# Expert weights of a one-core encoder step: 16 KB runs, rows turned by 64x64 products, ranks spread over the partitions

## What is computed

```python
def _hmoe(x, g, w_router_group, w_router_expert, w_gate, w_up, w_down):
    xn = _rmsnorm(x, g).reshape(b * l, dm)
    ...
    top_v, top_i = lax.top_k(le_sel, TOP_K_INNER)          # 2 of the 8 experts of the best group
    ...
    for e in range(N_EXPERTS):                             # 32
        h = jax.nn.silu(xn @ w_gate[e]) * (xn @ w_up[e])   # 1024 -> 512, twice
        y = y + combine[:, e:e + 1] * (h @ w_down[e]).astype(jnp.float32)   # 512 -> 1024
    return x + y.reshape(b, l, dm).astype(x.dtype)
```

## Time and profile before

| | |
|---|---|
| median of the runs | 861.42 us (861.15 to 863.01, 3 runs) |
| the profiled execution | 861.59 us |
| its span in the trace | 860.0 us |
| TensorE matmul busy | 776.5 us, 90% of the span |
| VectorE, ScalarE, GpSimd busy | 313.5, 137.5, 160.4 us |
| moved by DMA | 255.63 MB, mean 297 GB/s |
| queue q1 (SyncE's loads) | 237.04 MB |
| queue q0 (GpSimd's DMAs) | 17.43 MB |

### The profile page before, as it was taken

How to read it: one execution, slowest core, us unless ns; L and a number is a source line. 1 busy time by engine, 2 the same in 40 slices (tenths; PEclk the granted TensorE clock), 3 DMA queues, 4 the chain that set the end, 5 groups by cost and what they waited for, 6 DMA issues and landing times.

```text
span 860.0 us, 9611 instructions
## 1 busy us (share of the span) xinstructions
PE 776.5 (90%) x3720; PEld 428.1 (50%) x3721; DVE 313.5 (36%) x825; ACT 137.5 (16%) x275; POOL 160.4 (19%) x251
## 2 busy tenths in 40 slices
PE   4999999999999999999999878888789788789986
PEld 3888888787877455543333332333233233233332
DVE  4799879714474544551111110100101101101116
ACT  5110021222222323310000000000000000000023
POOL 4100018660133100020111010110100110101113
PEclk9999999999999999999999998989989999989998
DMA  9948033252500691589999999999999999999975
GB/s 277 314 158 141 2 112 77 79 227 101 196 1 1 270 420 75 205 331 415 424 419 420 423 421 421 424 420 423 421 421 424 421 421 422 422 422 403 401 281 234
DMA packets 59394, 255.63 MB, mean 297 GB/s; under 512 B 18272, under 2 KB 19124, under 8 KB 40660
## 3 DMA queue, kind: packets, MB, share of 16 engines
q1 hardware_dynamic: 50770, 237.04, 69.8%
q0 software_dynamic: 8160, 17.43, 5.5%
q10 hardware_dynamic: 418, 0.53, 0.3%
HBM read 243.70 MB, written 19.03 MB: 305 GB/s over the span
## 4 chain that ended last, share of the span: by engine, by line
PE 64%; DMA 29%; DVE 3%; issue 2%; ACT 1%; POOL 0%; SPq 0%; DVEq 0%; ACTq 0%; POOLq 0%
DMA arena<-in_w_exp_up 28%; PE ps L1907 15%; PE ps L1632 13%; PE ps L1695 11%; PE ps L1924 8%; PE ps L1792 6%; PE ps L1899 1%; PE ps L1881 1%; DMA arena<-in_x_prompt 1%; PE ps L1732 1%; PE ps L1725 1%; PE ps L1814 1%; PE ps L1916 1%; PE ps L1603 1%; PE ps L1804 0%
## 5 line engine op out<-in xcount | busy, mean ns | idle before, releaser
L1907 PE MATMUL ps<-arena 128*64 128x512 f32 x1024 | 247.2, 639 | 53.9 <-DMA arena<-in_w_exp_up 53.2
L1907 PEld LDWEIGHTS ps<-arena 128*64 128x64 f32 x1024 | 84.7, 146 | 194.7 <-issue 191.9
L1492 DVE TENSOR_TENSOR arena<-ps,arena 128x512 f32<-128x512 f32 x32 | 22.1, 692 | 283.1 <-PE ps L1899 283.1
L1924 PE MATMUL ps<-arena 128*64 128x512 f32 x512 | 118.6, 606 | 3.0 <-DVE arena L1526 3.0
L1632 PE MATMUL ps<-arena 128*128 128x272 f32 x480 | 110.8, 393 | 0.0
L1695 PE MATMUL ps<-arena 128*128 128x272 f32 x448 | 105.7, 394 | 2.1 <-DVE arena L1303 1.2
L686 POOL DMA_INDIRECT y_parts<-arena x31 | 31.1, 1002 | 377.5 <-DVE arena L1530 377.5
L1632 PEld LDWEIGHTS ps<-arena 128*128 128x128 f32 x480 | 91.0, 190 | 18.6
L1695 PEld LDWEIGHTS ps<-arena 128*128 128x128 f32 x448 | 83.8, 190 | 22.6 <-DVE arena L1303 2.9
L950 DVE TENSOR_TENSOR arena<-arena 128x256 f32<-128x256 f32 (+11 forms) x202 | 72.3, 358 | 13.0 <-ACT arena L853 3.9
L894 ACT ACTIVATE arena<-ps,arena 128x512 f32<-128x512 f32 x32 | 22.0, 687 | 299.2 <-PE ps L1907 299.2
(11 more groups left out here) (242 smaller groups left out, 571.9 us busy)
## 6 DMA issues: line engine op xcount, KB each, us to landing
arena<-in_w_exp_gate SPq DMA_DIRECT2D x28, 2048.0 KB, 37.0
arena<-in_w_exp_up SPq DMA_DIRECT2D x28, 2048.0 KB, 34.1
arena<-in_w_exp_down SPq DMA_DIRECT2D x27, 2048.0 KB, 38.5
arena<-in_w_in SPq DMA_DIRECT2D x6, 2048.0 KB, 9.1
arena<-in_w_exp_gate SPq DMA_DIRECT2D x16, 512.0 KB, 10.6
arena<-in_w_exp_up SPq DMA_DIRECT2D x16, 512.0 KB, 18.9
arena<-in_w_exp_down SPq DMA_DIRECT2D x6, 1024.0 KB, 19.4
arena<-in_x_prompt SPq DMA_DIRECT2D x8, 512.0 KB, 9.3
```

Of the source, the lines that this page charges most:

```text
L1907: last = pe.matmul(ps[n * TILE:(n + 1) * TILE, 2 + par, :], x_t[:, k, :], w[:, k, :], start=(k == 0), stop=(k == KD - 1))
L1924: last = pe.matmul(ps[half * TILE:(half + 1) * TILE, 6 + par, :], h[par][:, k, :], w_down[:, k, half * F:(half + 1) * F], start=(k == 0), ...
```

## The change

Five things, in one program:

1. **Gate and up in runs of 16 KB.** Partition p of the ring now holds rows 8p to 8p + 7, which lie next to each other in memory, so a whole load is one piece of 16 KB for each partition. Quarters are 4 KB pieces, as before. The scale vector `g_x` is loaded in the same order.
2. **Rows turned by 64x64 products.** With this order of rows, each half of the fetched rows goes to its own half of the partitions. `turn_x` is now 16 products with a 64x64 piece of the identity in place of four 128x128 transposes, and `x_out` reads and writes without a change of order.
3. **Ranks four partitions apart.** `slot_no` is filled by four iotas in place of one. Ranks 0 to 7 get slots 0, 4, ..., 28, ranks 8 to 15 slots 29, 25, ..., 1, ranks 16 to 31 the slots left of the first 32, ranks 32 on the second 32 in the same way.
4. **The eleventh load in quarters.** Load 10 goes out as four quarters, each when its token tile of `x_tok` has been stored, turned and squared: three between loads 6 and 7, the last where load 10 stood, behind the wait for `xg_in[0]`. GpSimd now waits for each store of rows before it issues the next.
5. **All pair sums on GpSimd.** Tile 3 joins `PAIRED`, TensorE adds one part in place of two.

The core of the diff:

```diff
-PAIRED = (4, 0, 1, 2)
+PAIRED = (4, 0, 1, 2, 3)
...
-    return l >= NS and held_before(l) // 3 < QUARTERED and held_before(l) % 3 != 2
+    return l == NS - 1 or l >= NS and held_before(l) // 3 < QUARTERED and held_before(l) % 3 != 2
...
-        experts = [a[f"w_exp_{n}"][0].rearrange("e (h p k) n -> e p h (k n)", h=h, p=P)
-                   for n, h in (("gate", 2), ("up", 2), ("down", 1))]
...
+        experts = [a[f"w_exp_{n}"][0].rearrange("e (p k) n -> e p (k n)", p=P) for n in ("gate", "up", "down")]
...
-            def load(l, c0=0, words=SLOT):
-                sp.dma_start(weight_place(l, c0, words), weight_rows(l // 3, l % 3, c0, words)).then_inc(w_arr[place(l)], 16)
+            def load(l, part=slice(0, SLOT)):
+                sp.dma_start(ring[place(l)][:, part], experts[l % 3][l // 3][:, part]).then_inc(w_arr[place(l)], 16)
...
+            def load_over(n):
+
+                sp.wait_ge(x2_stored, 16 * (n + 1))
+                sp.wait_ge(x2_turned, 2 * n + 2)
+                sp.wait_ge(squares, TT + 2 * n + 2)
+                q = OUT_ORDER[n]
+                load(NS - 1, slice(q * QUARTER, (q + 1) * QUARTER))
+
+            for n in range(1, TT - 1):
+                load_over(n)
...
             sp.wait_ge(xg_in[0], 16)
-            load(NS - 1)
+            load_over(TT - 1)
...
-            pool.iota(slot_no, pattern=[[0, 2], [1, TILE]], base=0, channel_multiplier=0,
-                      allow_small_or_imprecise_dtypes=True)
+            by_turn = slot_no.rearrange("p h (a j b o) -> p o h a j b", a=2, j=8, o=2)
+            for odd in range(2):
+                for k in range(2):
+                    pool.iota(by_turn[:, odd, k], pattern=[[32, 2], [-1 if odd else 1, 8], [16, 2]], base=15 * odd,
+                              channel_multiplier=0, allow_small_or_imprecise_dtypes=True)
...
                 pool.wait_ge(x2_ready, 2 * n + 2)
+                if n:
+                    pool.wait_ge(x2_stored, 16 * n)
...
-                dve.tensor_tensor(xg_t[par].rearrange("p (h k) t -> p k h t", h=2),
...
+                dve.tensor_tensor(xg_t[par], ps[:, par, :].rearrange("p (k t) -> p k t", k=KD),
+                                  g_x.unsqueeze(2).to_broadcast((P, KD, TILE)), ALU.mult).then_inc(xt_ready, 1)
...
-                blocks = rows[buf].rearrange("t (q k) -> t k q", k=4)
-                for k in range(4):
-                    last = pe.transpose(ps[:, bank, k * P:(k + 1) * P], blocks[:, k, :], ident)
+                blocks = rows[buf].rearrange("t (q k) -> t k q", k=KD)
+                for k in range(KD):
+                    for half in range(2):
+                        part = slice(half * TILE, (half + 1) * TILE)
+                        last = pe.matmul(ps[part, bank, k * TILE:(k + 1) * TILE], blocks[part, k, :], ident[part, part],
+                                         start=True, stop=True)
...
-                if i in PAIRED:
-                    pe.wait_ge(pair_sum, PAIRED.index(i) + 1)
-                else:
-                    pe.wait_ge(y_back[i], 16)
-                    add(i, y_end[i][:, D:2 * D], False)
-                add(i, y_end[i][:, 0:D], True).then_inc(sum_done, 1)
+                pe.wait_ge(pair_sum, PAIRED.index(i) + 1)
+                add(i, y_end[i][:, 0:D]).then_inc(sum_done, 1)
```

33 lines of the change are left out of this document (11 added, 22 removed).

## The result

| | before | after |
|---|---|---|
| median of the runs, us | 861.28 (861.11 to 863.01, 4 runs) | 868.34 (867.07 to 869.29, 4 runs) |
| profiled execution, us | 861.59 | 867.63 |
| its span, us | 860.0 | 866.0 |
| gate-up of expert 0 starts | 375.41 | 381.85 |
| gate-up of expert 28 starts | 781.91 | 782.58 |

The changed kernel is slower: ratio 1.0074, 95% interval 1.0062 to 1.0086. The forecast was 849.7 us, so it missed by 18.6 us and by its sign. The loss is under 1%, but the interval lies wholly above 1. In the spans the 6.0 us more are 0.67 up to the gate-up of expert 28, 4.15 from there to the last down product, 1.2 at the end.

The account below looks back on a forecast made before the run. Weight loads bound the kernel up to 781.9 us, then TensorE and the closing sums. 5 + 6 + 2.0 - 0.4 = 12.6 us gained, less 0.9 in the tail, gave 11.7 and 849.7 us, range 845.5 to 856.

Parts of the forecast that it names:

- Part 2: Turning of fetched rows on TensorE: 0.3 us more each, bounds 0.3 to 1.5; added instruction fetches 0.4 us on the weights.
- Rival A: Turning: halves sharing one PSUM bank don't overlap, 2.0 us for 32 matmuls, 855.7 us in all; chance 0.15.
- the slack of 3.8 us: TensorE's spare time per expert, steps of 15.79 against 12.03 us, claimed to hide the longer turning up to expert 28.
- Load 85: The up load of expert 28, where the weight-bound stretch ends: claimed to land 12.6 us earlier.
- The four iotas: Filling of the slot order on GpSimd: claimed to run while it waits for the first rows, costing nothing.
- The tail: From expert 28's gate-up on: three turnings on the path, 0.9 us longer, with the remaining loads in time.
- Part 5: Closing sums, the fifth moved to GpSimd: 0 us, bounds -1.6 to +1.6, since a small VectorE operation might be held.
- Part 3: Spread ranks even out the DMA engines' row work: 6 us earlier at expert 28's up load, bounds 0 to 7.3.
- Rival B: Spreading the ranks brings nothing, as the slowest engine's lag has another cause: 855.7 us; chance 0.07.
- Part 4: Eleventh load in quarters uses idle DMA time before the first experts: 2.0 us gained, bounds 0 and 3.7.
- Part 1: Gate and up loads in 16 KB runs: 5 us less on the weight stream, bounds 2.4 to 7.8.
- rival C: Runs of 16 KB bring nothing, the packet difference being chance: 854.7 us; chance 0.08.

Follow-up runs that it names:

- first_old: Changed kernel with whole-row turning products, late iotas and four sums, expert 0 alone turned by four 128x128 transposes (timing only): 857.85 us, ratio 0.9961.
- runs_alone: Kernel before with only the 16 KB runs and the new turning by 64x64 products: 869.16 us, ratio 1.0066.
- spread_and_quarters: Kernel before with spread ranks (iotas late) and the eleventh load in quarters, 8 KB runs and old turning kept: 855.51 us, ratio 0.9924.
- old_late_four: Changed kernel with the old turning by four 128x128 transposes, late iotas and four sums (timing only): 853.39 us, ratio 0.9891.
- column_late_four: Changed kernel with turning by products of whole 128-row weights, late iotas and four sums: 862.74 us, ratio 1.0003.
- old_turn: Changed kernel with only the turning as before, four 128x128 transposes (timing only), early iotas and five sums kept: 857.12 us, ratio 0.9941.
- two_banks: Changed kernel with the two halves of a turning in different PSUM banks, scaled by two VectorE operations: 869.87 us, ratio 1.0075.

## Why the prediction was wrong

**Part 2, the turning: the step that failed.** It failed in two places: the price of a turning, and what a longer turning does outside the tail. The sum took 0.3 us more for each turning, with 1.5 as the upper bound, from line 1677. That row fitted in columns, count and alternating halves, but its weights lie side by side, and those of the turning 32 bytes apart, which no row of line 1677 or 1732 has. With contiguous weights the estimate holds: 1.08 us against the forecast 1.0. As built it was 2.07 us, and the cost was 1.39 and not 0.3. Line 1732's 2.2 us, the upper end, was nearer by number but for another reason. The stride was in the diff (`k=KD` for `k=4` in the rearrangement), and the argument never spoke of it. But the right price alone would not have saved the forecast: the kernel with contiguous weights has it and takes 863.25 us, some 13 above the 849.7.

**Rival A** had the price, 2.0 us, and the wrong mechanism: different banks change nothing, so the rule on row tiles and banks (the Trainium skill, "TensorEngine Tiling (Array Packing)", PSUM pressure) doesn't set the time here. Its 855.7 us was too low also with that price.

**"Up to expert 28 the slack of 3.8 us hides it": false for the first 14 experts.** The slack is the difference of two paces, 15.8 against 12.0. It exists only once the ring's loads wait for the DMA engines. In the first experts it is the other way round: each freed place is a load that can start, and the slower TensorE is, the later it frees one. At 12.0 us for an expert the engines had all the work they could take from about 400 us on, at 13.35 us only from 450. The kernel before, then the changed one:

```profile
397.10:447.10 50.00, 50.00 (x236) 18.25 (x234) 7.47 (x12) 4.28 (x8) 9.09 (x9) 1.00 1.02 421
```

```profile
450.00:497.00 47.00, 47.00 (x308) 20.96 (x306) 5.93 (x10) 3.90 (x7) 6.83 (x7) 1.00 1.01 426
```

That is the 3.4 us lost between 400 and 450; at the 12.36 us of contiguous weights it is 0.5 (421 against 425).

**The start, not forecast at all.** The larger part, 8.3 us, is lost before 400 us, because the first gate-up is late and slow and so frees its places late. The scaling that waits for the first small products starts 2.2 us after their last record, and a stretch at half clock follows (9.27 us for 7.09). With the old turning neither happens, and 21.3 x (425 - 354) / 425 = 3.6 us are lost there:

```profile
379.30:400.60 21.30, 21.13 (x102) 7.97 (x100) 7.70 (x27) 2.14 (x4) 1.27 (x3) 1.00 0.98 354
```

So the new turning costs 8.3 - 3.6 = 4.7 us at the start, 3.4 by its pace and 4.2 in the tail, 12.3 in all, where the times give 11.5. Contiguous weights take away 2.9 us of the pace and 3.0 of the tail, but nothing of the start: that part comes with the small products and not with their stride (first_old prices it at 3.6 us in another kernel). The last store also takes 1.8 us longer beside loads with 16 KB packets (runs_alone; 0.6 to 1.9 over all kernels), ahead of the first gate-up as well.

**Load 85,** forecast 12.6 us earlier, comes out at -12.6 + (11.7 - 1.2) + 2.9 = 0.8 us later, with the forecast's own gains and 2.9 for what was left of load 10 (issued at 376.72 instead of 373.78). Measured are 0.67. The gain was made and spent in the first 120 us.

**"The four iotas for one run while GpSimd waits, nothing": false.** GpSimd waits, but only after it has released `route_consts`, and VectorE and TensorE wait for that. 0.85 us there, 1.4 more by the clock (5.02 us for 3.63), 2.2 us of the result.

**The tail.** Forecast 0.9 us longer; measured 4.15, which is 3 x 1.39. The count of three was right, the term was not.

**Part 5.** 0, bounds -1.6 to +1.6: 1.2 by the profile, within the bounds; VectorE was held not in a small operation but in the scaling of tile 4.

**Part 3, the spread: right at its place.** Forecast 6 us at load 85, measured 6.15 (0.7 of it already at the first gate-up). The moved bytes exceed the needed by 1.1 MB, not 0.5; in the changed kernel they are 118.3 x 383 + 285.6 x 425 = 166.7 MB against 165.8 needed (75.25 loads). The Trainium skill's swizzle ("DMA: Bandwidth & Descriptors", the descriptor swizzle) fits what the landings show, over 12 us apart before and 3.5 to 4.4 with spread ranks. Rival B falls. But only 3.9 us reached the end: that the tail follows in full was wrong by two products at half clock, less one that the kernel before has.

**Part 4: right**, 2.4 us against 2.0, with bounds 0 and 3.7.

**Part 1: right in sign, small.** Forecast 5, bounds 2.4 to 7.8. spread_and_quarters and old_late_four differ by this alone (and by where the x values stand): 2.8 us of time; the gate-up of expert 28 gains 1.9 although the first starts 1.6 later, so 3.5 on the weights, if a later start shifts all that follows. With the 15.65 against 15.80 us of runs_alone and the faster stream this speaks against rival C, but each of these differences is small.

**Together,** in ratios times 861.3 us, the forecast missed by 18.0 (1.0074 against 849.7 / 861.3 = 0.9865). The turning cost 11.5 where 0.9 and 0.4 were forecast, 10.2 of the miss (9.6 us is its cost by column_late_four against old_late_four). Iotas and fifth sum cost 4.3 together where nothing was forecast (old_turn against old_late_four). The parts that were to gain gave 9.4 us (old_late_four) where 5 + 6 + 2.0 = 13.0 were forecast, 3.6 of the miss. Of 0.97 for faster, nearly all rested on one row that matched in everything but the stride, on one word, "hidden", and on a start that was taken as unchanged. The Trainium skill's note on the lines of the on-chip memory ("SBUF — State Buffer", Door 1), which bears on the stride, wasn't weighed.

## What to carry over

Before a weight layout is made longer in memory, ask what it forces on the operand that meets it: 8 KB more in a run gained 2.8 us, and the turning it forced cost three to four times that, 4.7 us of it by loads 32 bytes apart and most of the rest by a late first gate-up. When one cause is found, repair it alone and see how much of the loss goes: here it was less than half. A slack between two paces hides nothing in the first turns of a ring, where the consumer decides when transfers can start. And one instruction more ahead of a semaphore counts by who waits for that semaphore, not by how idle its own engine is.

## What was not expected of the hardware

- A weight load of 64 float32 columns takes 212 ns with its elements 32 bytes apart and 134 ns side by side; 32 of them, two halves at a time, make 2.07 and 1.08 us.
- The first turning by small products (64 columns of weights, 64 moved) let the scaling behind it start 1.3 to 3.4 us after its last record in eight kernels, 0.4 us after it in a ninth (two_banks), and 0.1 us where small products had run just before. Transposes of 128x128 didn't show this (seven kernels). Its cause is open.
- A stretch at half clock costs a product group about 1.7 us (8.72 for 7.09, 5.35 for 3.65). How many fall into the tail differs from kernel to kernel, and with spread ranks alone it took back about a third of what they had gained at load 85.
- The last row store takes 9.9 to 10.8 us to land beside loads in 8 KB packets (four kernels) and 11.4 to 11.8 beside 16 KB packets (thirteen kernels).
